# Expert layers: raw blocks in other places, and a twelfth buffer for picked rows

## The reference

```python
def peer_ffn(x, norm_g, q_w, sub_keys, u, v):
    h = rmsnorm(x, norm_g).reshape(T, D)
    q = (h @ q_w).reshape(T, PEER_HEADS, 2, PEER_HALF)
    s = jnp.einsum('thcd,ckd->thck', q, sub_keys).astype(jnp.float32)
    s1, i1 = lax.top_k(s[:, :, 0], PEER_TOPK)
    s2, i2 = lax.top_k(s[:, :, 1], PEER_TOPK)
    ...
    best_s, best_pos = lax.top_k(cand_s, PEER_TOPK)
    idx = jnp.take_along_axis(cand_i, best_pos, axis=-1)
    gate = jax.nn.softmax(best_s, axis=-1).astype(x.dtype)
    ...
        a = jnp.einsum('nd,nhkd->nhk', hb, u[ib])
        w = gb * jax.nn.gelu(a, approximate=False)
        return jnp.einsum('nhk,nhkd->nd', w, v[ib])
```

## Time and profile before

| | us |
|---|---|
| median of 3 runs (2741.81 to 2745.07) | 2744.03 |
| profiled execution, its own time | 2741.04 |
| span of its trace | 2739.2 |

### The profile page before, as it was taken

How to read it: one execution, slowest core, us unless ns; L and a number is a source line. 1 busy time by engine, 2 the same in 40 slices (tenths; PEclk the granted TensorE clock), 3 DMA queues, 4 the chain that set the end, 5 groups by cost and what they waited for, 6 DMA issues and landing times.

```text
span 2739.2 us, 32208 instructions
## 1 busy us (share of the span) xinstructions
PE 2461.3 (90%) x10416; PEld 1678.3 (61%) x10416; DVE 1915.0 (70%) x3841; ACT 1178.3 (43%) x2586; POOL 855.8 (31%) x700
## 2 busy tenths in 40 slices
PE   8999999999989999998998787789988998777688
PEld 7888788888778877986544333334765454333244
DVE  7885588888768875654676767666667676776675
ACT  4446744444564456563333333333453333323334
POOL 0005400000230026754333333444433333333442
PEclk9999999999999999999999889999999999999999
DMA  6654365556425553448999999999639999999996
GB/s 209 189 180 139 117 198 190 172 192 190 158 70 195 188 163 127 165 142 331 420 418 421 417 419 415 414 414 420 205 142 413 420 421 421 417 420 417 411 414 265
DMA packets 142240, 783.39 MB, mean 286 GB/s; under 512 B 15904, under 2 KB 16416, under 8 KB 76576
## 3 DMA queue, kind: packets, MB, share of 16 engines
q0 software_dynamic: 73728, 536.90, 47.4%
q1 hardware_dynamic: 65648, 237.45, 26.1%
q10 hardware_dynamic: 2736, 7.46, 0.9%
HBM read 780.69 MB, written 1.05 MB: 285 GB/s over the span
## 4 chain that ended last, share of the span: by engine, by line
PE 48%; DMA 22%; issue 9%; DVE 8%; ACT 7%; POOL 6%; another core or an unknown queue 0%; POOLq 0%; ACTq 0%; SPq 0%; DVEq 0%
DMA arena<-experts,arena 22%; PE ps L717 11%; PE ps L1300 6%; PE ps L1303 6%; PE ps L718 6%; PE ps L695 5%; PE ps L696 5%; PE ps L697 5%; POOL ring_lo L401 4%; DVE arena L2723 2%; ACT row L1912 2%; POOL arena L2840 1%; PE ps L1258 1%; ACT arena L1905 1%; ACT L1903 1%
## 5 line engine op out<-in xcount | busy, mean ns | idle before, releaser
L2723 DVE SCALAR_TENSOR_TENSOR arena<-arena,ps 128x1024 f32<-128x1024 f32 x512 | 616.4, 1219 | 370.3 <-DMA arena<-experts,arena 354.0
L1300 PE MATMUL ps<-arena,row 128*128 128x512 f32 x1024 | 568.3, 638 | 197.3 <-ACT row L1912 190.3
L2840 POOL DMA_INDIRECT arena<-experts,arena x512 | 485.3, 948 | 761.4 <-PE ps L1303 508.9
L1303 PE MATMUL ps<-arena,row 128*128 128x512 f32 x1024 | 549.7, 620 | 0.0
L717 PE MATMUL ps<-hT,ring_hi 128*128 128x512 f32 x1408 | 503.4, 400 | 2.9 <-DVE hT L2239 2.7
L394 ACT ACTIVATE ring_hi<-ring 128x1024 fp32r<-128x1024 f32 x408 | 429.8, 1058 | 172.4 <-PE ps L697 127.4
L1300 PEld LDWEIGHTS ps<-arena,row 128*128 128x128 f32 x1024 | 198.2, 202 | 474.5 <-ACT row L1912 259.5
L401 POOL TENSOR_TENSOR ring_lo<-ring,ring_hi 128x1024 fp32r<-128x1024 f32 x139 | 334.5, 2416 | 235.0 <-ACT ring_hi L394 212.7
L718 PE MATMUL ps<-hT,ring_lo 128*128 128x256 f32 x1408 | 395.9, 281 | 0.0
L1303 PEld LDWEIGHTS ps<-arena,row 128*128 128x128 f32 x1024 | 205.5, 201 | 266.4 <-issue 266.4
L401 DVE TENSOR_TENSOR ring_lo<-ring,ring_hi 128x1024 fp32r<-128x1024 f32 x269 | 324.1, 1228 | 18.3 <-ACT ring_hi L394 17.6
(11 more groups left out here) (350 smaller groups left out, 3599.4 us busy)
## 6 DMA issues: line engine op xcount, KB each, us to landing
ring<-stream SPq DMA_DIRECT2D x424, 512.0 KB
arena<-experts,arena POOLq DMA_INDIRECT x512
row<-rows_in ACTq DMA_DIRECT2D x11, 512.0 KB, 5.2
arena<-stream SPq DMA_DIRECT2D x8, 512.0 KB, 5.8
queries_in_ring_hi<-stream SPq DMA_DIRECT2D x8, 512.0 KB
queries_in_w<-stream SPq DMA_DIRECT2D x4, 512.0 KB, 7.8
queries_in_h_lo<-stream SPq DMA_DIRECT2D x4, 512.0 KB, 5.3
x<-x_in SPq DMA_DIRECT2D x1, 1024.0 KB, 5.3
```

The costliest lines, as they stand in the source:

```text
L1300: lower = pe.matmul(ps[:, 2 * tb, :], diag, v[:, 0:HALF], start=first, stop=end)
L1303: pe.matmul(ps[:, 2 * tb + 1, :], diag, v[:, HALF:D], start=first, stop=end)\
L2723: last = dve.scalar_tensor_tensor(u, u, 1.0, h, ALU.mult, ALU.mult, accum_out=R["a"][:, n % 2, k:k + 1])
L2840: pool.indirect_dma_start(R["held"][:, g % HELD, :], None, experts, bass.IndirectOffsetOnAxis(ap=idx[:, n % 2, k:k + 1], axis=0))\
```

## The change

The query blocks get other places: 2 and 3 in what will be buffer 10 of the arena, 4 and 5 in `w`, 6 and 7 in `s`, 8 and 9 as before, 10 to 13 in the ring, 14 in a free end of the arena, 15 in `ring_hi`. The four blocks behind them (`AHEAD`) are loaded raw into `ring_lo` as soon as the last four projection blocks of the layer before have been used, and are split in place later. Gates 2 and 3 follow when queries 12 and 13 have been used. `w` becomes a twelfth buffer for picks, number 11, so a pick waits for the one 12 before it. Since buffers 10 and 11 first hold queries 2 and 3, and 4 and 5, pick 10 of a layer waits until `used` shows query 3 done, and pick 11 until it shows query 5 done.

```diff
-HELD = 11
+HELD = 12
+IN_ARENA = 11
+QUERIES_IN_RING = (12, 13, 10, 11)
+QUERIES_LOADED = ((0, 1, 4, 5), (8, 9, 2, 3, 6, 7, 14))
+AHEAD = {AT[f"peer{l}_q"] + SUBS + i: l for l in range(2) for i in range(SLOTS)}
...
         def raw(b):
-            l, m = QUERY.get(b, (0, SLOTS))
+            l, m = QUERY.get(b, (0, SUBS))
+            if b in AHEAD:
+                return blocks_in_ring_lo[:, b % SLOTS, :]
+            if m in QUERIES_IN_RING or m == SUBS:
+                return ring[:, b % RING, :]
             if m < 2:
                 return region(0, 2, BLK)[0][:, m, :]
...
+            if m < 4:
+                return split(peer_regions()["held"][:, IN_ARENA - 1, :], 2, BLK)[:, m - 2, :]
+            if m < 6:
+                return queries_in_w[:, m - 4, :]
...
+        def held(g):
+            if slot_of(g) < IN_ARENA:
+                return peer_regions()["held"][:, slot_of(g), :]
+            return queries_in_w.rearrange("p m c -> p (m c)")
...
+                    sp.wait_ge(used, AT["swa_out" if l else "ssm_out"])
+                    load(8, 10)
...
+                    load(2, 4)
+                    load(6, 8)
+                    load(14, 15)
+                    for n, m in enumerate(QUERIES_IN_RING):
+                        who, own = SPLIT[b - SLOTS + n][1:]
                         sp.wait_ge(lo_ready[who], own + 1)
+                        load(m, m + 1)
+                    for n in range(SLOTS):
+                        sp.wait_ge(used, b - SLOTS + n + 1)
+                        load(SUBS + n, SUBS + n + 1)
+                    load(SUBS - 1, SUBS)
+                    for n in range(2):
+                        sp.wait_ge(used, b + QUERIES_IN_RING[n] + 1)
+                        load(SUBS + SLOTS + n, SUBS + SLOTS + n + 1)
...
                         if g >= HELD:
-                            pool.wait_ge(of("expert_free"), g - HELD + 1)
-                        pool.indirect_dma_start(R["held"][:, g % HELD, :], None, experts,
+                            pool.wait_ge(of("expert_free"), max(g - HELD + 1, PICKS * l))
+                        if n == 0 and k == IN_ARENA - 1:
+                            pool.wait_ge(used, base + 4)
+                        if n == 0 and k == IN_ARENA:
+                            pool.wait_ge(used, base + 6)
+                        pool.indirect_dma_start(held(g), None, experts,
```

More of the change, by code:

```diff
@@ L317, in peer_regions @@
                        limit=HELD_AT)
-            r["held"], _ = region(HELD_AT, HELD, EXPERT)
+            r["held"], _ = region(HELD_AT, IN_ARENA, EXPERT)
             r["q0"] = r["cand"]
@@ new lines, in raw, with in_ring, loaded_with @@
+            return region(SPACE - BLK, BLK)[0] if m == 14 else queries_in_ring_hi[:, b % SLOTS, :]
+        def in_ring(b):
+            return b not in AHEAD and (b not in QUERY or QUERY[b][1] in QUERIES_IN_RING)
+        def turns_before(b):
+            return sum(in_ring(earlier) for earlier in range(b % RING, b, RING))
+        def loaded_with(b):
+            m = QUERY[b][1] if b in QUERY else SUBS
+            for n, blocks in enumerate(QUERIES_LOADED):
+                if m in blocks:
+                    return n, len(blocks)
+            return len(QUERIES_LOADED), 1 + SLOTS
@@ new lines, in raw_loaded, with slot_of, landings @@
+        def raw_loaded(b):
+            return loaded[b % RING] if in_ring(b) else of(f"queries_loaded{loaded_with(b)[0]}")
+        def slot_of(g):
+            return g % PICKS % HELD
+        def held(g):
+            if slot_of(g) < IN_ARENA:
+                return peer_regions()["held"][:, slot_of(g), :]
+            return queries_in_w.rearrange("p m c -> p (m c)")
+        def landings(g):
+            return 16 * (g // PICKS * len(range(slot_of(g), PICKS, HELD)) + g % PICKS // HELD + 1)
@@ L553, in _, with load @@
-                    continue
-                if b in NEXT_IN_RING:
-                    sp.wait_ge(used, NEXT_IN_RING[b] + 1)
-                    sp.dma_start(raw(b), stream[b]).then_inc(raw_loaded(b), 16)
-                    b += 1
+                    l = QUERY[b][0]
+                    def load(first, end, base=b):
+                        for m in range(first, end):
+                            sp.dma_start(raw(base + m), stream[base + m]).then_inc(raw_loaded(base + m), 16)
+                    sp.wait_ge(used, AT["swa_out" if l else "ssm_out"])
@@ L564, in _ @@
                     pick_of = HELD_BACK[b]
-                    sp.wait_ge(expert_landed[pick_of % HELD], 16 * (pick_of // HELD + 1))
+                    sp.wait_ge(expert_landed[slot_of(pick_of)], landings(pick_of))
                 first = b - RING + 1 if way == "used" else SPLIT[b - RING][2] + 1
@@ L2720, in dots @@
                         g = PICKS * l + TOPK * n + k
-                        u = R["held"][:, g % HELD, 0:D]
-                        dve.wait_ge(expert_landed[g % HELD], 16 * (g // HELD + 1))
+                        u = held(g)[:, 0:D]
+                        dve.wait_ge(expert_landed[slot_of(g)], landings(g))
                         last = dve.scalar_tensor_tensor(u, u, 1.0, h, ALU.mult, ALU.mult,
```

55 lines of the change are left out of this document (16 added, 39 removed).

## The result

| | before | after |
|---|---|---|
| median of the runs | 2744.28 us (4 runs, 2741.81 to 2745.07) | 2765.16 us (4 runs, 2763.58 to 2767.06) |
| ratio, 95% interval | | 1.0078 [1.006, 1.0095] |
| profiled execution, span | 2741.04, 2739.2 | 2767.06, 2765.2 |

The changed kernel is 20.9 us slower, by the interval 16.5 to 26.1 us; 23.7 us were forecast. Its median of 2765.16 us lies in the forecast's inner range, 2764 to 2772.

The account below looks back on a forecast made before the run. The DMA engines were taken to bound both expert layers. +31.2 us for late pick 11 less 7.5 for blocks gave +23.7: 2764.7 for the profiled execution, about 2768 us median; inner range 2764 to 2772, full range 2757 to 2776.

Parts of the forecast that it names:

- The main term: Start of each expert layer: pick 11 waits for query 5, the DMA queue runs empty; both layers together +31.2 us.
- The 6.40 us: Step from POOL's gather end to DVE's start, read at unit 13, taken for a gather finding the queue almost empty.
- The second layer: Second expert layer's start: pick 11 usable at 2102.58 in place of 2086.78, 15.8 us later.
- Both holes: Delays of pick 11 at the starts of the two layers, 15.4 and 15.8 us, together +31.2 us.
- No second hole: At pick 16 the list of experts comes 0.6 us in time; if late, up to 2 us a layer more.
- The blocks out of the gathers: Ring loads leave the gather phase; three per layer count at 1.25 us each, -7.5 us over two layers.
- query 15: One block more at the gather phase's start, taken by the hole behind pick 10: 0 us.
- The blocks put ahead: Three more arena blocks loaded before the gathers; their 3.75 us fit into the empty DMA time soon after: 0.
- the sub-keys: Before each layer: their load taken as not delayed, 0; rival (8%): up to 3.75 us late, +31.2 us, 2775.
- The twelfth buffer: Expert layers: taken as 0, the list holds POOL at unit starts; rival (6%): it pays, +14.5 us, 2758.5.
- the 4.6 us a layer: Expert layers: 0.7% of 648 us that deeper queueing could win, kept as the other end of the twelfth buffer's 0.
- The sum: Whole kernel: +31.2 - 7.5 = +23.7 us; second phase starts about 12 us late and ends about 24 us late.

Follow-up runs that it names:

- e1: Changed kernel with eleven buffers again and no wait of pick 11 for query 5, blocks in their new places: 2736.59 us, kernel before 2741.31.
- e2: Changed kernel, twelve buffers, with queries 0 and 1 in `w` and 4 and 5 in the arena: 2735.20 us, kernel before 2741.31.
- e5: e1 (eleven buffers) with DVE computing the next unit's list of experts ahead of the group 2 dot products: 2734.59 us, kernel before 2740.52.
- e6: e2 (twelve buffers) with DVE computing the next unit's list of experts ahead of the group 2 dot products: 2733.72 us, kernel before 2740.52.
- e3: Kernel before, its buffers and places kept, with one added wait of pick 11 for query 5: 2765.60 us, without the wait 2741.31.
- e4: Kernel before, its buffers and places kept, with one added wait of pick 11 for query 4: 2741.46 us, without the wait 2741.31.
- e9: e6 with the four held-back gate blocks of each layer released four picks sooner: 2741.85 us, kernel before 2740.43.
- e10: e2, with its late list, and the four held-back gate blocks of each layer released four picks sooner: 2744.25 us, kernel before 2740.43.

## Why the prediction was right, and where its sizes were off

**The main term.** Right in mechanism, place and sign. Pick 11 was forecast at about 1310 in the first layer, and at 2095 in the second before the 12 us by which that layer was to start late; released by PE's query product, it left at 1310.01 and 2108.27. The DMA share was forecast below a third in 1295 to 1310 and was 0.14, and 0.09 in the second layer. DVE's pick 11 came 1315.58 - 1302.02 = 13.6 us late in the first layer, where 15.4 were forecast; the term was mis-sized by the step from POOL's end to DVE's start. The 6.40 us came from the start of unit 13, at 1798. The prediction took the queue for almost empty there; it was not: after POOL's gather had left, DVE still waited for two earlier gathers, landed at 1799.79 and 1802.29, and the one at 1804.78 came 2.49 us behind them, the usual spacing. Behind a drained queue it is 1315.58 - 1310.95 = 4.63 us, and 2113.76 - 2109.20 = 4.56 us in the second layer. By the estimate from the Trainium skill ("DMA: Bandwidth & Descriptors", Anatomy of one DMA), 4.4 us, this step would have been right to 0.2 us; the trace now agrees with the page.

**The second layer.** Forecast 15.8 us late, beyond a shift of its start; measured 2113.76 - 2086.78 - 10.75 = 16.2 us, 10.75 being how much later the first gather came (2060.68 against 2049.93). With the step as measured it would be 14.0. The other 2.2 us: counted from the first gather, query 5 started 43.19 us behind it and not 41.41 (1.8 us, of which 1.1 in the row of queries 2 and 3, 9.49 us and not 8.43), and POOL started 0.78 us after the release and not 0.28. Both holes: 29.8 us against 31.2.

**No second hole.** Right in effect: the list was ready at 1319.60 + 0.17 = 1319.77 and not 1321.6, 4.2 us after pick 11 as forecast, and pick 16 left at 1320.05. DVE took it at 1329.26, and 1329.84 was forecast. Two misses cancel in that: the step of 4.63 us was shorter than forecast, and the five picks behind pick 11 took 1.3 us more than five spacings of 2.48 us, in both layers. Why they do is open.

**The blocks out of the gathers.** Forecast -7.5 us; e1 measured -4.7 [-7.7, -3.0], e2 with the buffer -6.1. The direction and the mechanism stand. In e1 and e2 some 3 us are given back by query 15 and the crowded start, for which the prediction had 0: from the first gather's issue to its first packet it takes 4.0 and 4.2 us in the two layers, and 2.6 in both layers before. In the changed kernel the same delay is there (4.0 and 4.2 us), but the hole takes it, as forecast; what is missing there of the 7.5 us (2.2 us) is about the 1.3 us a layer behind pick 11.

**The blocks put ahead, and the sub-keys.** The 0 for the sub-keys was right. The first layer's first gather was issued at 1265.37, and at 1265.41 before; the second layer's came 127.4 us behind the last packet of the first layer's gathers, and 127.2 us before. That rival is out.

**The twelfth buffer.** The 0 was right (e1 against e2), the reason only in part. The list did hold POOL; taking that away (e5, e6) brought about 1 us, inside the uncertainty, since the pauses it made were hardly in the 16th raises. So the 4.6 us a layer that the prediction kept as a bound are not to be had by deeper queueing or by an earlier list. The rule cited from "Perfetto Trace Analysis" in the Trainium skill (Optimization Strategy), that repeated gaps on the saturated engine can mean too few buffers, is not the case here: with one buffer more (e2), and with the wait for the list nearly gone as well (e6), the time is the same within about 1 us.

**The sum.** DVE's last pick of the first layer comes 10.5 us later than before (1933.78 against 1923.25), that of the second 24.5 us (2732.96 against 2708.42); 12 and 24 were forecast. That is 29.8 us of holes less 5.3 for the blocks, where 31.2 less 7.5 were forecast: the sum came out nearer than its terms, by luck. The two profiled executions differ by 26.0 us, the medians by 20.9: the profiled one is the slowest of four after the change and the fastest of four before it. The forecast of 23.7 lies between.

**What stays open.** Which DMA engines lag and why. A difference of 1.5 us behind the last landing, in several kernels: 31.3 us before and in e2, at a mean granted clock of 0.93 and 0.94, and 32.8 us after and in e1, at 0.91 and 0.92. And why query 5 stands where it does. In the traces of the kernel before and of the changed one, ACT stands idle for 6 to 7.4 us near the start of each expert layer, ended by nothing that the profile knows of this core:

```profile
1276.81 0.28 ACT L1903 ACTIVATE pick<-ps 128x128 f32<-128x128 f32 x1 [6.00 <-remote]
```

In e3 the same idle is 1.65 us, ended by PE. So PE starts query 5 40.7 and 43.2 us after the layer's first gather in the changed kernel, and 40.8 and 41.4 us before, but 37.2 and 37.5 us in e3 and 37.2 us in both layers of e4. A late query 5 is a longer hole: 13.6 and 16.2 us in the changed kernel, 11.4 and 11.8 us in e3. Whether the changed kernel would lose less without that idle was not run.

## What to carry to other kernels

A wait put between two transfers costs nothing while the transfers already issued cover it, and what lies beyond is lost: count the issued transfers by the landing spacing, and look up where the releasing instruction stands in its own engine's list. When a buffer is to be shared, let the reader that is done first lie in it: the kernel with the twelfth buffer was some 27 us slower with queries 4 and 5 in it than with queries 0 and 1, or than with queries 4 and 5 computed ahead of the first unit. A price read from one row holds for the state of that row; a drained queue and one with two gathers under way differ here by 1.8 us.

## What the runs showed of the hardware

- A 1 MB indirect gather behind a drained queue was usable on DVE 4.6 us after POOL's instruction ended; in the earlier trace rows, behind two gathers still landing, it was 6.4 us, and in e3, with ring loads in the hole, 5.5 and 5.8 us.
- The 16 raises of one gather's semaphore lie about 2 us apart at a layer's start. With pauses in the issue (e2) that stays so, 2.6 and 2.9 us at its end; with hardly any (e6) it grows to 7.7 and 7.3 us. The 16th raises come each 2.48 us either way.
- With the queue always full, the mean DMA share and the landings tell different things: 119 GB/s in a window of e6 (1911 to 1915) in which picks landed each 2.48 us all the same, as at 420 GB/s.
- Eight blocks of 512 KB (four a layer), moved four picks ahead, cost 8.2 us in e9 and 9.9 us in e10, 1.0 to 1.2 us each: about their bytes at 420 GB/s (1.25 us), though in e9 the engines were mostly idle (a share of 0.19 from 1915 to 1920).
- After 9.56 us of idle TensorE's granted clock was 0.55 (1316 to 1326), and a pair of matmuls took 2.08 us where it takes 1.02 us; the DMA engines moved 424 GB/s meanwhile.
